# A two-block transformer kernel: Silu tiles that wait for the slots they overwrite, a time-step chain moved up, another order in the first pair, and products of constants in four waits

## The chip, the cores and the metric

The kernel runs on one core of one Trainium2 chip. The metric is device time in microseconds, median of the runs. All data is float32. The engines are named as the profile names them: PE multiplies matrices (PEld is its loading of weights), DVE and POOL do elementwise work, ACT evaluates functions, SP issues most DMAs.

## The reference

512 latent tokens and 256 context tokens of width 1024 go through two blocks. The first has two layers: a hybrid mixer (attention beside a state-space scan in two directions) and a gated feed-forward, then a short convolution and a second feed-forward. The second block has an RWKV-7 mix beside dilated attention, a cross attention to a memory, and a last feed-forward. The parts that the change touches:

```python
def ssd_mixer(p, conv_w, conv_b, dt_bias, a_log, d_skip, ssm_norm, h0_f, h0_b):
    z = p[..., IDX_Z:IDX_XBC]
    xbc = jax.nn.silu(dw_conv(p[..., IDX_XBC:IDX_DT], conv_w, conv_b))
    ...
    dt = jax.nn.softplus(p[..., IDX_DT:].astype(jnp.float32).reshape(b, t, 2, SSM_HEADS)
                         + dt_bias.astype(jnp.float32))
    a = -jnp.exp(a_log.astype(jnp.float32))

def ssd_scan(xs, dt, a, bm, cm, h0):
    ...
    a_cs = jnp.cumsum(dtc * a.astype(f32).reshape(g, e), axis=2).transpose(0, 3, 4, 1, 2)
    xdt = x * dtc[..., None]
    cb = jnp.einsum('bclgn,bcsgn->bcgls', cc, bc)
    y_diag = jnp.einsum('bcgls,bgecls,bcsgep->bclgep', cb, segsum_exp(a_cs), xdt)
    decay_to_end = jnp.exp(a_cs[..., -1:] - a_cs)
    ...

def rwkv7_mix(p_r, p_k, p_v, p_wd, p_ad, p_gd, w0, w2, a0, a2, g2, k_k, k_a, r_k, gn_w, gn_b):
    ...
    kk = kk / jnp.maximum(jnp.sqrt(jnp.sum(kk * kk, axis=-1, keepdims=True)), 1e-12)
    k = p_k * (1.0 + (a - 1.0) * k_a)
    y = rwkv7_scan(r, decay, k, v, -kk, kk * a)
    ...
    bonus = (jnp.sum(r * k * r_k, axis=-1, keepdims=True) * v).reshape(B, S, RWKV_DIM)
```

## The kernel before, in words

Everything is one function, `two_blocks`, with one hand-written program per engine. An engine runs its program in order; a wait names another engine's step (a counter that a `prog` object keeps), so the order of lines is the order of work, and an engine that waits holds up all that stands behind it. Weights come through a ring of four slots that SP fills ahead.

**Attention loop and state-space lead.** Attention takes 16 steps (4 head pairs by 4 query tiles). Between its own operations each step carries fill: PE does projections, DVE convolves tiles of the state-space input (`convolution`, six tiles of 768 columns) and multiplies rows of the modulation weights (`ada_unit`, L2574, 80 units; their rows arrive in four slots named AW). PE sums each finished block of ten (`block_sums`, L1317), DVE adds a bias (`block_mod`, L2585). Behind the loop comes the lead of the state-space scan. ACT applies Silu to the six convolved tiles (L2222 and L2223, steps s0 to s5). Their destination XS lies on the memory of the AW slots, so before the change all six wait for the last `block_mod`, "b9". Then, all in ACT's order: Silu of the gate z (L2225); the exponentials and the logarithm of the softplus (L2229, L2231, L2233); half of the copies of the transposed tiles (L2236, L2239); the exponentials of the decay sums, dte and dcy (L2241, L2242). DVE has the other steps of softplus (L2683 to L2694: u, d, r, ru, corr, pos; then sp, dt and dta to L2703), its own copies (L2709), the masked products CBM (L2713) and the decay sums (L2716 to L2722). PE waits for s5, then transposes the tiles (tx, L1378; tb, L1383), multiplies the B and C parts (cb, L1392), sums the decays (acs, L1398; tot, L1401) and starts the scan proper with `running` (L1438). POOL moves B and C to other partitions by four DMAs (L1080, after s5).

**First RWKV pair.** Eight head pairs go one after the other. Most of what pair i needs is made during pair i-1; the first has to make it itself (DVE L2973 to L3010): shift mixes, the norm of the keys (nmax, ninv, nk: L2984 to L2988), the decay sums (cs, t, km: L2993 to L2997), the decayed operands (bb, rt, at0, at, bt, kt: L2999 to L3007) and the input of the bonus (rk, L3010). PE waits for rk and then transposes (tr, L1682), makes the gram products, part of a projection (L1636) and the first level of an inverse (p0, L1725). POOL multiplies the grams by level masks (L1123) for p0. Before the first pair POOL also scales the eight tiles of X by `rstd` (L1112), which DVE makes by a reciprocal (L3020) after rk.

**Four places where PE waits for DVE or ACT.** Before the output projection of the hybrid mixer PE waits for the normalized group "y1" (L1502). Behind `scaled_pe` (L748) in the two feed-forwards and in the short convolution it waits for the fourth low part of the normalized input, "l3", and later for "l7" (L848). Before the last feed-forward's second product it waits for the first hidden tiles (`ff2_products`, L833).

Of the kernel before, what the change touches and what calls it, by code (L numbers as in the profile page):

```python
# [295 lines left out]
def two_blocks(nc, a, consts_d, bias_d, out):  # L296

    ctx = ExitStack()
    with ctx:
# [204 lines left out]
        ss_pe = prog("ss_pe", " ".join(f"tx{c}" for c in range(NA)) + " tb0 tb1 cb0 cb1 acs tot")  # L504
# [638 lines left out]
        def _(pe):  # L1143
# [250 lines left out]
            pe.wait_ge(dt_dve.sem, dt_dve.done("dta"))  # L1394
            pe.wait_ge(ss_dve.sem, ss_dve.done("tx3"))
            flat = lambda x: x.rearrange("p d c h -> p d (c h)")
            for d in range(2):
                mm = nc.tensor.matmul(bank[3][:, d * 48:(d + 1) * 48], const["tri_b" if d else "tri_f"], flat(DT["dta"])[:, d, :],  # L1398
                                      start=True, stop=True)
            mm.then_inc(ss_pe.sem, ss_pe.step("acs"))  # L1400
            nc.tensor.matmul(bank[3][:, 96:192], ONES, DT["dta"].rearrange("p d c h -> p (d c h)"),  # L1401
                                        start=True, stop=True).then_inc(ss_pe.sem, ss_pe.step("tot"))
# [1883 lines left out]
```

## Time and profile before

| | us |
|---|---|
| median of 3 runs | 2822.73 |
| lowest and highest | 2822.01, 2824.67 |
| the profiled execution | 2820.58 |
| its span in the trace | 2818.8 |
| PE busy | 2709.2 (96%) |
| share of the chain that ended last | PE 83%, DVE 3%, issue 1%, ACT 1% |

Busy time is summed over instructions of an engine. The chain is followed back from the last instruction to what released each step. PEclk, in the windows view, is the clock that TensorE was granted, as a share of full speed (1.00 is 2.4 GHz, 0.50 is 1.2 GHz). In a timeline, the bracket at the end of a line is the idle time of the engine before that instruction and the engine, tile and line that ended it.

### The profile page before, as it was taken

Reading aid. Unit: us, or ns where it says so; the run is one execution under the profiler, and the core shown is the slowest. Engines: PE = TensorE matmul, PEld = TensorE weight load, DVE = VectorE, ACT = ScalarE, POOL = GpSimd, SP = SyncE. Lnnn points to the kernel's source line nnn. Section 1 sums busy time; section 2 is a strip of 40 time slices with the busy share of each in tenths; the row PEclk is TensorE's granted clock in tenths of the full one; section 3 lists DMA queues with packets and bytes.
Section 4 is the critical chain, followed back from the end, with each engine's and each line's share of the span. In section 5 each row is a group of like instructions: output and inputs, shape, how many; then the busy total and the mean of one; then the engine's idle time right before and its main releaser. Section 6 shows DMA issues by size and latency. Waiting matters only on the chain.

```text
span 2818.8 us, 43450 instructions
## 1 busy us (share of the span) xinstructions
PE 2709.2 (96%) x17761; PEld 1956.3 (69%) x17761; DVE 1663.6 (59%) x2208; ACT 655.8 (23%) x1138; POOL 202.9 (7%) x219
## 2 busy tenths in 40 slices
PE   7899799999999999999989999999989999999998
PEld 4555455888878878888645555575667788788887
DVE  4788676555456665554456666654365675655554
ACT  4233433111010021110133333232341211211102
POOL 2000231000000010000031111110000000100001
PEclk9999899999999999999999999999999999999999
DMA  7475302333323323333211211112123333233332
GB/s 256 150 260 189 100 23 82 97 89 95 95 86 97 90 86 93 97 93 95 70 38 34 58 42 34 34 57 65 43 56 89 91 106 111 68 97 94 93 96 74
DMA packets 394393, 255.53 MB, mean 91 GB/s; under 512 B 19767, under 2 KB 376720, under 8 KB 394128
## 3 DMA queue, kind: packets, MB, share of 16 engines
q1 hardware_dynamic: 391456, 246.78, 29.6%
q0 software_dynamic: 2320, 5.11, 0.6%
q8 instruction: 107, 1.75, 0.3%
q10 hardware_dynamic: 480, 1.64, 0.2%
q14 instruction: 30, 0.25, 0.0%
HBM read 250.61 MB, written 2.10 MB: 90 GB/s over the span
## 4 chain that ended last, share of the span: by engine, by line
PE 83%; DVE 3%; issue 1%; ACT 1%; POOL 0%; DVEq 0%; ACTq 0%; POOLq 0%
PE PS L833 15%; PE PS L834 15%; PE PS L835 15%; PE PS L1636 5%; PE PS L849 3%; PE PS L848 3%; PE PS L1611 3%; PE PS L850 3%; PE PS L1725 1%; PE PS L1617 1%; PE PS L1421 1%; PE PS L1502 1%; PE PS L1841 1%; PE PS L1863 1%; PE PS L1751 1%
## 5 line engine op out<-in xcount | busy, mean ns | idle before, releaser
L859 DVE CAST WH<-W 128x1024 fp32r<-128x1024 f32 x304 | 213.4, 702 | 419.0 <-PE PS L835 373.2
L834 PE MATMUL PS<-XNL,WH 128*128 128x512 f32 x960 | 381.8, 398 | 0.0
L861 DVE TENSOR_TENSOR WL<-W,WH 128x1024 fp32r<-128x1024 f32 x304 | 374.5, 1232 | 10.4
L833 PE MATMUL PS<-HH,WH 128*128 128x512 f32 x672 | 262.1, 390 | 0.2 <-DVE HL L2934 0.2
L834 PE MATMUL PS<-HL,WH 128*128 128x512 f32 x672 | 261.5, 389 | 0.0
L835 PE MATMUL PS<-HH,WL 128*128 128x512 f32 x672 | 261.5, 389 | 0.0
L834 PEld LDWEIGHTS PS<-XNL,WH 128*128 128x128 f32 x960 | 180.8, 188 | 41.6 <-issue 0.5
L833 PE MATMUL PS<-XNH,WH 128*128 128x512 f32 x512 | 202.2, 395 | 0.0
L835 PE MATMUL PS<-XNH,WL 128*128 128x512 f32 x512 | 201.3, 393 | 0.0
L833 PE MATMUL PS<-XN2H,WH 128*128 128x512 f32 x448 | 178.6, 399 | 11.4 <-issue 7.5
L835 PE MATMUL PS<-XN2H,WL 128*128 128x512 f32 x448 | 177.5, 396 | 0.0
L1636 PE MATMUL PS<-HXF,W 128*128 128x512 f32 x336 | 165.6, 619 | 0.0
L848 PE MATMUL PS<-XNH,WH 128*128 128x512 f32 x384 | 154.1, 401 | 10.4 <-DVE XNL L779 10.4
L849 PE MATMUL PS<-XNL,WH 128*128 128x512 f32 x384 | 154.0, 401 | 0.0
L850 PE MATMUL PS<-XNH,WL 128*128 128x512 f32 x384 | 152.7, 398 | 0.0
L833 PEld LDWEIGHTS PS<-HH,WH 128*128 128x128 f32 x672 | 126.1, 188 | 28.1 <-DVE HL L3253 1.3
L835 PEld LDWEIGHTS PS<-HH,WL 128*128 128x128 f32 x672 | 126.1, 188 | 26.3
L834 PEld LDWEIGHTS PS<-HL,WH 128*128 128x128 f32 x672 | 126.1, 188 | 26.0
L3043 DVE TENSOR_TENSOR ARENA<-ARENA,PS 128x512 f32<-128x512 f32 (+1 forms) x80 | 48.0, 632 | 117.2 <-PE PS L1753 116.9
L833 PEld LDWEIGHTS PS<-XNH,WH 128*128 128x128 f32 x512 | 96.3, 188 | 23.7 <-issue 0.2
L835 PEld LDWEIGHTS PS<-XNH,WL 128*128 128x128 f32 x512 | 96.2, 188 | 23.0
L833 PEld LDWEIGHTS PS<-XN2H,WH 128*128 128x128 f32 x448 | 85.0, 190 | 35.4 <-issue 15.4
(516 smaller groups left out, 4639.2 us busy)
## 6 DMA issues: line engine op xcount, KB each, us to landing
ARENA<-in_ada_w SPq DMA_DIRECT2D x80, 512.0 KB, 5.3
W<-in_ffn_w SPq DMA_DIRECT2D x64, 512.0 KB, 4.0
W<-in_w_in SPq DMA_DIRECT2D x51, 512.0 KB, 4.0
W<-in_ffn_w_gate SPq DMA_DIRECT2D x44, 512.0 KB, 3.8
W<-in_ffn_w_up SPq DMA_DIRECT2D x44, 512.0 KB, 3.8
W<-in_ffn_w_down SPq DMA_DIRECT2D x32, 512.0 KB, 4.0
W<-in_sc_w_in SPq DMA_DIRECT2D x24, 512.0 KB, 3.8
ARENA<-in_ada_w SPq DMA_DIRECT2D x8, 1024.0 KB, 18.3
```

The costliest lines, as they stand in the source:

```text
L833: nc.tensor.matmul(dst, WH[:, h, c], hi(k), start=(start and k == 0), stop=False)
L834: nc.tensor.matmul(dst, WH[:, h, c], lo(k), start=False, stop=False)
L835: mm = nc.tensor.matmul(dst, WL[:, h, c], hi(k), start=False, stop=(stop and k == kts - 1))
L848: nc.tensor.matmul(dst[u], WH[:, h, c], hi(k), start=(k == 0), stop=False)
L849: nc.tensor.matmul(dst[u], WH[:, h, c], lo(k), start=False, stop=False)
L850: mm = nc.tensor.matmul(dst[u], WL[:, h, c], hi(k), start=False, stop=(k == KD - 1))
L859: nc.vector.tensor_copy(WH[:, h, :], W[:, s, 0:D]).then_inc(parted, 1)
L861: nc.vector.tensor_tensor(WL[:, h, :], W[:, s, 0:D], WH[:, h, :], ALU.subtract).then_inc(freed[s], 1)
L1421: mm = nc.tensor.matmul(bank[6 + o], tiles(sl)[:, NPAIR * o + k, :], MIX[:, k, :], start=(k == 0), stop=(k == NPAIR - 1))
L1611: return nc.tensor.matmul(bank[7], w, xn(k), start=(k == 0), stop=(k == KD - 1))
L1636: mm = nc.tensor.matmul(bank[7], tiles(s)[:, k, :], xn(k), start=(k == 0), stop=(k == KD - 1))
L3043: tt(own, own, PS[:, 2 + 2 * e + first:4 + 2 * e, 0:NT * CHUNK], ALU.add).then_inc(p_dve.sem, p_dve.step(f"z{l}{e}"))
```

## The change

It has three parts.

In the lead, each Silu tile waits for the AW slots that it overwrites (all their uses done) in place of "b9". Tiles 0 to 2 stand ahead of the copy of the last pair's attention output on ACT, 3 to 5 behind it. The softplus chain is spread over the loop: its first DVE steps stand behind the first row maximum, two exponentials on ACT in step 14, six DVE steps and the logarithm in step 15, the rest before the last `block_mod`. PE makes acs and tot, in another bank, before the last `block_sums`; the first transposes wait for s3 alone.

```diff
-        ss_pe = prog("ss_pe", " ".join(f"tx{c}" for c in range(NA)) + " tb0 tb1 cb0 cb1 acs tot")
+        ss_pe = prog("ss_pe", "acs tot " + " ".join(f"tx{c}" for c in range(NA)) + " tb0 tb1 cb0 cb1")
...
+            pe.wait_ge(dt_dve.sem, dt_dve.done("dta"))
+            flat = lambda x: x.rearrange("p d c h -> p d (c h)")
+            for d in range(2):
+                mm = nc.tensor.matmul(bank[7][:, d * 48:(d + 1) * 48], const["tri_b" if d else "tri_f"], flat(DT["dta"])[:, d, :],
+                                      start=True, stop=True)
+            mm.then_inc(ss_pe.sem, ss_pe.step("acs"))
...
             for b in ended(STEPS):
                 block_sums(b, NPAIR)
-            pe.wait_ge(cv_act.sem, cv_act.done(f"s{XBC_TILES - 1}"))
-            pe.wait_ge(at_act.sem, at_act.done(f"o{NPAIR - 1}"))
-            pe.wait_ge(blocks_dve.sem, blocks_dve.done(f"b{len(ADA_BLOCKS) - 1}"))
+            pe.wait_ge(cv_act.sem, cv_act.done(f"s{NPAIR - 1}"))
...
+            def conv_out(j):
+                act.wait_ge(cv_dve.sem, cv_dve.done(f"c{j}"))
+                for u in range(TA * j // D, min((TA * (j + 1) - 1) // D + 1, AW_SLOTS)):
+                    act.wait_ge(aw_used[u], KD * len(ADA_BLOCKS) // AW_SLOTS)
+                nc.scalar.activation(XS[:, j, 0:T], CONV[j][:, 0:T], ACT.Silu, bias=col("conv_b", j))
+                nc.scalar.activation(XS[:, j, T:TA], CONV[j][:, T + 2:TA + 2], ACT.Silu, bias=col("conv_b", j)).then_inc(cv_act.sem, cv_act.step(f"s{j}"))
...
+                if g == STEPS - 1:
+                    act.wait_ge(dt_dve.sem, dt_dve.done("u"))
+                    nc.scalar.activation(act_flat("l"), act_flat("u"), ACT.Ln).then_inc(dt_act.sem, dt_act.step("l"))
+                    act.wait_ge(at_dve.sem, at_dve.done(f"p{STEPS - 1}1"))
+                    for j in range(XBC_TILES // 2):
+                        conv_out(j)
```

On ACT, at the end of the attention loop, this stood in a row before (L2216 copies the last pair's attention output, L2222 and L2223 are Silu of one tile, L2225 Silu of the gate, L2229 to L2233 the softplus, L2236 and L2239 copies of transposed tiles, L2241 and L2242 dte and dcy):

```order
L2222 ACTIVATE ARENA<-ARENA,COLS 128x512
L2223 ACTIVATE ARENA<-ARENA,COLS 128x256
L2225 ACTIVATE ARENA<-ARENA 128x2048
L2229 ACT_TABLE_LOAD
L2229 ACTIVATE ARENA<-ARENA 128x16
L2231 ACTIVATE ARENA<-ARENA 128x96
L2233 ACT_TABLE_LOAD
L2233 ACTIVATE ARENA<-ARENA 128x96
L2236 ACTIVATE HXF<-PS 128x512 x3
L2239 ACTIVATE ARENA<-PS 128x512
L2239 ACTIVATE ARENA<-PS 128x256
L2241 ACT_TABLE_LOAD
```

and this stands there now (L2247 the logarithm, L2216 and L2217 Silu of tiles 2 and 3, L2253 the copy of the attention output, L2258 Silu of the gate, L2261 and L2262 dte and dcy, L2265 copies):

```order
L2247 ACT_TABLE_LOAD
L2247 ACTIVATE ARENA<-ARENA 128x96
L2216 ACT_TABLE_LOAD
...
L2216 ACTIVATE ARENA<-ARENA,COLS 128x512
L2217 ACTIVATE ARENA<-ARENA,COLS 128x256
L2253 ACTIVATE ARENA<-PS 128x512
L2216 ACTIVATE ARENA<-ARENA,COLS 128x512
L2217 ACTIVATE ARENA<-ARENA,COLS 128x256
...
L2258 ACTIVATE ARENA<-ARENA 128x2048
L2261 ACT_TABLE_LOAD
L2261 ACTIVATE ARENA<-ARENA 128x96
L2262 ACTIVATE ARENA<-PS 128x96
L2265 ACTIVATE HXF<-PS 128x512 x3
```

The softplus and two table loads are gone from behind the Silu tiles, and dte and dcy stand ahead of the copies. On PE the same place read before (L1348 values of the last pair):

```order
L1348 MATMUL PS<-ARENA 64x512 x12
L1317 MATMUL PS<-CONST,ARENA 128x2 x8
L1378 MATMUL PS<-CONST,ARENA 128x128 x24
L1383 MATMUL PS<-CONST,ARENA 128x128 x6
L1392 MATMUL PS<-HXF 128x128 x8
L1398 MATMUL PS<-ARENA,CONST 128x48 x2
L1401 MATMUL PS<-ARENA,CONST 128x96
L1438 MATMUL PS<-ARENA,CONST 128x512 x2
```

and now:

```order
L1352 MATMUL PS<-ARENA 64x512 x12
L1377 MATMUL PS<-ARENA,CONST 128x48 x2
L1380 MATMUL PS<-ARENA,CONST 128x96
L1321 MATMUL PS<-CONST,ARENA 128x2 x8
L1388 MATMUL PS<-CONST,ARENA 128x128 x24
L1396 MATMUL PS<-CONST,ARENA 128x128 x6
L1405 MATMUL PS<-HXF 128x128 x8
L1443 MATMUL PS<-ARENA,CONST 128x512 x2
```

The two decay sums moved from behind the B and C products to ahead of the block sums.

In the first RWKV pair, DVE makes cs, t and km ahead of the key norm, PE's transposes wait for kt in place of rk, and `rstd` goes to a place of its own in DIL0, so that POOL can scale X later: one tile behind each pair's level masks.

```diff
-            pool.wait_ge(one_dve.sem, one_dve.done("rstd"))
-            for k in range(KD):
-                nc.gpsimd.tensor_tensor(X[:, k, :], X[:, k, :], YR[:, 2, :], ALU.mult).then_inc(one_pool.sem, one_pool.step(f"x{k}"))
+            def scaled(k):
+                pool.wait_ge(one_dve.sem, one_dve.done("rstd"))
+                nc.gpsimd.tensor_tensor(X[:, k, :], X[:, k, :], DIL0[:, 7, :], ALU.mult).then_inc(one_pool.sem, one_pool.step(f"x{k}"))
...
-            with pool.Fori(0, RW_PAIRS - 1) as i:
+            for i in range(RW_PAIRS - 1):
                 level_masks(i, i, rw_pe, rw_dve, rw_pool)
+                scaled(i)
+            for k in range(RW_PAIRS - 1, KD):
+                scaled(k)
...
                 if i == 0:
-                    pe.wait_ge(rf_dve.sem, rf_dve.done("rk"))
+                    pe.wait_ge(rf_dve.sem, rf_dve.done("kt"))
...
+            decay_sums(0, 0, rf_act, rf_dve)
             key_norm(0, rf_act, rf_dve)
-            decayed(0, 0, rf_act, rf_dve)
+            decayed(0, rf_act, rf_dve)
```

POOL's order at the first pair was (L1109 sums, L1112 scales a tile of X, L1123 a level mask inside a loop of seven pairs):

```order
L1109 TENSOR_TENSOR ARENA<-ARENA 128x512 x6
L1112 TENSOR_TENSOR X<-X,ARENA 128x512 x8
L1126 UNCONDITIONAL_BRANCH
L1126 ISA
L1120 ISA
L1123 TENSOR_TENSOR ARENA<-ARENA,CONST 128x256
```

and is, without the loop:

```order
L1109 TENSOR_TENSOR ARENA<-ARENA 128x512 x6
L1124 TENSOR_TENSOR ARENA<-ARENA,CONST 128x256 x10
L1113 TENSOR_TENSOR X<-X,ARENA 128x512
L1124 TENSOR_TENSOR ARENA<-ARENA,CONST 128x256 x10
L1113 TENSOR_TENSOR X<-X,ARENA 128x512
```

All eight scalings have left the place ahead of the first pair's masks.

Third, PE gets products of constants whose results nobody reads, into banks that are free there: six before the wait for y1, six behind `scaled_pe` in each feed-forward and in the short convolution, seven before the last feed-forward's second product. Each is a float32 product of 512 columns, which PE runs as two halves.

```diff
+            def warm(b, n):
+                for _ in range(n):
+                    nc.tensor.matmul(bank[b], ONES, const["chunk_reset"], start=True, stop=True)
...
+            warm(2, 6)
             pe.wait_ge(gn_dve.sem, gn_dve.done("y1"))
...
                 scaled_pe(pe, norm_ffn[layer], SQ_MIX2, 6)
+                warm(5, 6)
...
             scaled_pe(pe, norm_sc, SQ_MIX2, 6)
+            warm(7, 6)
...
+            warm(3, 7)
             ff2_products(0, True)
```

## Rows read from the trace of the kernel before

**Rows 1.** Page, part 1: busy us, share of the span and instructions of each engine.
```profile
PE 2709.2 (96%) x17761; PEld 1956.3 (69%) x17761; DVE 1663.6 (59%) x2208; ACT 655.8 (23%) x1138; POOL 202.9 (7%) x219
```
**Rows 2.** Timeline of PE in the lead: start, us, engine, line, op, count, idle before.
```profile
305.28 1.95 PE L1317 MATMUL PS<-CONST,ARENA 128*128 128x2 f32 x16 [0.69 <-ACT ARENA L2216]
315.02 5.38 PE L1378 MATMUL PS<-CONST,ARENA 128*128 128x128 f32 x24 [7.79 <-ACT ARENA L2223]
...
322.46 2.02 PE L1392 MATMUL PS<-HXF 64*128 64x128 f32 x16 [0.99 <-DVE HXF L2709]
...
327.19 3.78 PE L1438 MATMUL PS<-ARENA,CONST 128*128 128x512 f32 x4 [1.26 <-ACT ARENA L2242]
```
**Rows 3.** Timeline of ACT in the lead.
```profile
296.97 0.81 ACT L2203 ACTIVATE ARENA<-PS 128x768 f32<-128x768 f32 x1 [1.70 <-PE PS L1306]
...
307.50 1.28 ACT L2222 ACT_TABLE_LOAD   x1 [2.27 <-DVE MOD L2585]
308.80 0.72 ACT L2222 ACTIVATE ARENA<-ARENA,COLS 128x512 f32<-128x512 f32 x1
...
314.87 1.89 ACT L2225 ACTIVATE ARENA<-ARENA 128x2048 f32<-128x2048 f32 x1
```
**Rows 4.** Timeline of DVE in the lead.
```profile
296.55 4.05 DVE L2574 SCALAR_TENSOR_TENSOR ARENA<-ARENA,SILU_C 128x1024 f32<-128x1024 f32 x3
...
323.63 2.48 DVE L2713 TENSOR_TENSOR ARENA<-PS,CONST 128x512 f32<-128x512 f32 x4
```
**Rows 5.** Timeline of POOL in the lead; then the tile view of HXF, from issue to landing.
```profile
315.57 2.09 POOL L1080 DMA_DIRECT2D HXF<-ARENA  x4 [297.49 <-ACT ARENA L2223]
...
DMA to landing us min/median/max: 2.6/3.6/4.1
```
**Rows 6.** Windows: us, then PE, PEld, DVE, ACT, POOL busy (instructions), PEclk, DMA share, GB/s.
```profile
302.00:307.00 5.00, 4.31 (x30) 2.33 (x24) 0.00 (x0) 0.60 (x1) 0.00 (x0) 1.00 0.36 87
315.00:321.00 6.00, 5.98 (x28) 5.98 (x29) 2.19 (x8) 5.94 (x9) 2.09 (x4) 0.50 0.53 131
318.50:320.70 2.20, 2.20 (x12) 2.20 (x12) 1.92 (x7) 2.19 (x4) 0.00 (x0) 0.50 0.64 168
```
**Rows 7.** Timeline of DVE in the first RWKV pair.
```profile
1431.31 0.43 DVE L2984 TENSOR_SCALAR RSTD<-ROOT 128x512 f32<-128x512 f32 x1 [2.69 <-ACT ROOT L2321]
...
1435.77 1.22 DVE L2993 TENSOR_TENSOR_SCAN ARENA<-CONST,ARENA 128x512 f32<-128x512 f32 x1
...
1438.01 0.69 DVE L2999 SCALAR_TENSOR_TENSOR ARENA<-ARENA 128x512 f32<-128x512 f32 x1
...
1441.22 0.75 DVE L3010 SCALAR_TENSOR_TENSOR ARENA<-ARENA,COLS 128x512 f32<-128x512 f32 x1
...
1451.99 1.75 DVE L3036 TENSOR_TENSOR ARENA<-ARENA,CONST 128x512 f32<-128x512 f32 x1
```
**Rows 8.** Timeline of PE: the first pair, and the transposes of the second and third.
```profile
1442.02 3.67 PE L1682 MATMUL PS<-CONST,ARENA 128*128 128x128 f32 x16 [4.68 <-DVE ARENA L3010]
...
1456.73 1.38 PE L1725 MATMUL PS<-ARENA 64*64 64x64 f32 x32 [2.78 <-POOL ARENA L1123]
...
1511.02 1.91 PE L1682 MATMUL PS<-CONST,ARENA 128*128 128x128 f32 x16
...
1572.76 1.91 PE L1682 MATMUL PS<-CONST,ARENA 128*128 128x128 f32 x16
```
**Rows 9.** Timeline of POOL in the first pair.
```profile
1445.31 10.77 POOL L1112 TENSOR_TENSOR X<-X,ARENA 128x512 f32<-128x512 f32 x8 [20.61 <-DVE ARENA L3020]
```
**Rows 10.** Timeline of PE at the waits that get products of constants.
```profile
416.72 3.65 PE L1502 MATMUL PS<-ARENA,W 128*128 128x512 f32 x4 [3.55 <-DVE ARENA L2735]
...
454.54 0.76 PE L848 MATMUL PS<-XNH,WH 128*128 128x512 f32 x1 [3.46 <-DVE XNL L779]
...
459.51 0.50 PE L848 MATMUL PS<-XNH,WH 128*128 128x512 f32 x1 [0.29 <-DVE XNL L779]
...
2449.37 0.76 PE L833 MATMUL PS<-XN2H,WH 128*128 128x512 f32 x1 [3.88 <-DVE XNL L753]
```

More of the change, by code:

```diff
@@ L1369, in _ @@
                     values(g // NT)
+            pe.wait_ge(dt_dve.sem, dt_dve.done("dta"))
[4 more added lines that the diff above has]
+            mm.then_inc(ss_pe.sem, ss_pe.step("acs"))
+            nc.tensor.matmul(bank[7][:, 96:192], ONES, DT["dta"].rearrange("p d c h -> p (d c h)"),
+                                        start=True, stop=True).then_inc(ss_pe.sem, ss_pe.step("tot"))
             for b in ended(STEPS):
                 block_sums(b, NPAIR)
-            pe.wait_ge(cv_act.sem, cv_act.done(f"s{XBC_TILES - 1}"))
-            pe.wait_ge(at_act.sem, at_act.done(f"o{NPAIR - 1}"))
-            pe.wait_ge(blocks_dve.sem, blocks_dve.done(f"b{len(ADA_BLOCKS) - 1}"))
+            pe.wait_ge(cv_act.sem, cv_act.done(f"s{NPAIR - 1}"))
             for c in range(NA):
@@ L1380, in _ @@
             for c in range(NA):
+                if c == 0:
+                    pe.wait_ge(cv_act.sem, cv_act.done(f"s{NPAIR}"))
+                    pe.wait_ge(blocks_dve.sem, blocks_dve.done(f"b{len(ADA_BLOCKS) - 1}"))
                 if c == 4:
@@ L1393, in _ @@
                 mm.then_inc(ss_pe.sem, ss_pe.step(f"cb{g}"))
-            pe.wait_ge(dt_dve.sem, dt_dve.done("dta"))
             pe.wait_ge(ss_dve.sem, ss_dve.done("tx3"))
[L1396 to L1402, printed above, removed]
             pe.wait_ge(dt_act.sem, dt_act.done("dcy"))
@@ L1736, in pair_pass @@
                     if l == 4:
+                        if i == 0:
+                            pe.wait_ge(rf_dve.sem, rf_dve.done("rk"))
                         if ahead:
@@ L2198, in _ @@
                     exps(g + 1)
+                if g + 2 == STEPS:
+                    act.wait_ge(dt_in, 48)
+                    nc.scalar.activation(ALOG, ALOG, ACT.Exp).then_inc(dt_act.sem, dt_act.step("aexp"))
+                    act.wait_ge(dt_dve.sem, dt_dve.done("abs"))
+                    nc.scalar.activation(act_flat("e"), act_flat("abs"), ACT.Exp).then_inc(dt_act.sem, dt_act.step("e"))
                 for e in range(2):
@@ L2239, in _ @@
                 nc.scalar.activation(BTOK[:, 4 * n:4 * n + w, :], bank[b][:, 0:w * P].rearrange("p (c t) -> p c t", t=P), ACT.Copy).then_inc(ss_act.sem, ss_act.step(f"tb{n}"))
-            act.wait_ge(dt_dve.sem, dt_dve.done("tot"))
-            nc.scalar.activation(act_flat("dte"), act_flat("corr"), ACT.Exp).then_inc(dt_act.sem, dt_act.step("dte"))
-            nc.scalar.activation(act_flat("dcy"), bank[3][:, 96:192], ACT.Exp).then_inc(dt_act.sem, dt_act.step("dcy"))
             def group_square(j):
@@ L2706, in _ @@
             dve.wait_ge(dt_dve.sem, dt_dve.done("dta"))
+            dve.wait_ge(ss_pe.sem, ss_pe.done("tot"))
+            nc.vector.tensor_copy(fl("acs"), bank[7][:, 0:96]).then_inc(dt_dve.sem, dt_dve.step("acs"))
+            dve.wait_ge(dt_dve.sem, dt_dve.done("acs"))
+            ts(fl("neg"), fl("acs"), -1.0, None, ALU.mult).then_inc(dt_dve.sem, dt_dve.step("less"))
+            tt(fl("corr"), bank[7][:, 96:192], fl("acs"), ALU.subtract).then_inc(dt_dve.sem, dt_dve.step("tot"))
+            dve.wait_ge(dt_dve.sem, dt_dve.done("tot"))
+            for b in ended(STEPS):
+                block_mod(b)
             for c in range(1, NA, 2):
@@ L2714, in _ @@
                 ins.then_inc(ss_dve.sem, ss_dve.step(f"cb{g}"))
-            dve.wait_ge(ss_pe.sem, ss_pe.done("tot"))
-            nc.vector.tensor_copy(fl("acs"), bank[3][:, 0:96]).then_inc(dt_dve.sem, dt_dve.step("acs"))
-            dve.wait_ge(dt_dve.sem, dt_dve.done("acs"))
-            ts(fl("neg"), fl("acs"), -1.0, None, ALU.mult).then_inc(dt_dve.sem, dt_dve.step("less"))
-            tt(fl("corr"), bank[3][:, 96:192], fl("acs"), ALU.subtract).then_inc(dt_dve.sem, dt_dve.step("tot"))
-            dve.wait_ge(dt_dve.sem, dt_dve.done("tot"))
             dve.wait_ge(dt_act.sem, dt_act.done("dcy"))
```

86 lines of the change are left out of this document (42 added, 44 removed).

## The prediction, made before the changed kernel ran

> **What bounds the kernel now.** I read the page's first part, then the chain of waits, then engine timelines around the touched places, and for each place the granted clock. PE is busy 96% of the span, ACT 23% [rows 1], so only places where PE stands still can give much, and what another engine saves counts only if PE waits for it. There are three sorts here. In the lead, PE finishes its block sums at 305.28 + 1.95 = 307.2, stands 7.79 us until the last Silu tile, and starts the scan (`running`) at 327.19 after a short row of dependent steps [rows 2]. At the first RWKV pair it stands 4.68 us for rk, and 2.78 us before p0 for POOL's mask [rows 8]. At the five places where constant products go in, it stands 3 to 4 us each [rows 10]; of these rows the feed-forward's stands for three places alike (two feed-forwards and the short convolution).
>
> **Part 1, the lead.** The Silu tiles start at 308.80, behind a table load that began when DVE's block_mod (b9) ended [rows 3]. Six tiles take 314.87 - 308.80 = 6.07, 1.01 each. ACT's previous operation ended at 296.97 + 0.81 = 297.8, so nearly 10 us were there to use.
>
> Now I lay the new order on the same clock. The logarithm goes behind 297.8: a table load of 1.28 and about 0.3 (an estimate from the 0.27 per small operation below), so 299.4; the next load, for Silu, ends at 300.7. On DVE six softplus steps stand ahead of the last three rows of modulation: in the window of rows 6 that holds them seven small operations are busy 1.92, 0.27 each, with their gaps 2.1 for six. The rows, which ended at 296.55 + 4.05 = 300.6 [rows 4], end at 302.7. Tiles 0 and 1 overwrite slots that are free by 301.4 (a row is 1.35), tile 2 waits for the third of these rows at the latest, so tile 2 is done at 303.7. Then comes the copy that released the block sums at 305.28 (PE waited 0.69 for it [rows 2], thus a copy of some 0.6 from 304.6). It is not delayed, with 0.9 to spare. Tiles 3, 4 and 5 end at 306.2, 307.3 and 308.3.
>
> PE: dta is ready at 302.7 + 3 or 4 small steps = 303.7, so acs and tot start when the values end, 304.6. Before the change they filled PE from the end of cb (322.46 + 2.02 = 324.48) to the start of its 1.26 us wait for `running` (325.93) [rows 2], so 1.45. Then the block sums, 1.95, to 308.0; by then s3 is there, so the transposes start at 308.0 in place of 315.02 with no wait at all. Between 302 and 307 the clock was at 1.00 [rows 6], and PE no longer stops, so I take full speed: 28 of the 30 took 5.98 at 0.50 in 315 to 321 [rows 6]; all 30 at full speed are 3.2, so tx and tb end near 311.2, the last two of tb a little later, because ACT must first copy tx0.
>
> That copy stands behind the gate's Silu (308.3 + 1.89), a table load and two small exponentials: 312.0. Later than all this are the four DMAs of POOL. They began 0.7 after the last Silu tile made way for the gate's [rows 3, 5]; their issue takes 2.09 and landing 2.6 to 4.1 [rows 5]. From s5 at 308.3 this gives 309.0 + 2.09 + 2.6 = 313.7 at the earliest and 315.2 at the latest; the landing of an earlier one can hide in the issue of the next, so I take 313.7. The cb products, 2.02, end at 315.7, and DVE's masked products, 2.48 for four from 323.63 on, ended 326.11 - 324.48 = 1.6 behind cb before [rows 2, 4]. So `running` can start at 317.3 where it was 327.19: **9.9 saved**. What follows keeps its distances, since dte, dcy and the copies are ready earlier still.
>
> What loses its cover: the two exponentials in step 14 and the four small DVE steps at the start of the loop are 0.27 each. ACT is idle most of the loop, DVE stands there waiting for its first exponential; 0 to 1.6 us, I take 0. The most the lead gives: 11.8, if PE also runs `running` at full speed (3.78 for four halves at low clock, 1.9 at full). The least: 7.3 or 5, in the first two rivals.
>
> **Part 2, the first pair.** cs, t and km took 1438.01 - 1435.77 = 2.24 between nk and bb; DVE stood 2.69 before nmax [rows 7], and their inputs are there earlier than the root. So bb starts 2.24 sooner. kt ends where rk starts, 0.6 before the transposes began (1441.22 against 1442.02, less the signal): together the transposes start 2.24 + 0.6 = 2.84 sooner, at 1439.2. Then POOL: eight scalings of 10.77 [rows 9] stood ahead of the first mask, which released p0 at 1456.73. Without them, the pair has no reason to be longer than the next: from the transposes to the next transposes, 1572.76 - 1511.02 = 61.74, against 1511.02 - 1442.02 = 69.00 in the first. That is 7.26 more, **10.1 in all**. The scalings, 1.35 each, fall behind each pair's last mask, when POOL has nothing else for most of the pair; `rstd` must be ready only then. Price 0, at most the third rival's.
>
> **Part 3, constant products.** One half of 512 columns is 3.65/4 = 0.91 at low clock [rows 10], 0.46 at full. Twelve halves are 5.5 against a stand of 3.55, so y1's consumer starts 1.95 late. But it starts at full clock: its four halves cost 1.8 where they cost 3.65. Sum -0.1 to 0.1. In the feed-forwards and the short convolution they end 5.5 - 3.46 = 2.0 late, and PE there soon waits for l7 again: at 459.51 it stood 0.29 for DVE [rows 10], so a late start that catches up by its faster clock ends at the same moment. Three times 0. Before the last feed-forward 14 halves, 6.4 against 3.88: 2.5 late, with as much to win back from the cold clock (0.76 for its first matmul). Sum of part 3: **0**; bounds: -2, if the faster clock carries further, and +10.7, if none of the clock comes back (5.5 - 3.55, three times 2.0, and 2.5, to 10.5). It lies near 0 because the clock at 1.00 before each place is what the products find.
>
> **Sum.** 9.9 + 10.1 + 0 = 20.0 off the profiled execution's 2820.58: 2800.6. The median stands 2.15 above that execution, so I give **2802.7**.
>
> **Rivals.** *The clock is low where I took it full.* In the lead it stayed at 0.50 through six us of transposes [rows 6], after a stand, and I have no row with thirty transposes behind matmuls. At low clock tx and tb take 6.4, to 314.4, cb ends between 316.4 (full) and 318.4 (low), `running` starts 1.6 later, so the lead gives 9.2 to 7.2. In the pair, PE still stands about 2 us (1442.02 - 4.68 to 1439.2); if the clock falls there, the transposes take 3.67 in place of 1.91 [rows 8] and some grams behind them are slow too, 2.6 in all (estimate). Together 14.7 to 16.7 in place of 20.0: 2806 to 2808, I say 2807. For it: the low row. Against it: the sixteen transposes at 1.91 in the later pairs, behind matmuls. The Trainium skill, "TensorE: Matmul & The Clock Gate", section "Part 4: PE-mode transpose", says that transposes do not count as busy PE, so that the fast clock does not engage for them; by that rule the time would be the one of this rival, some 4 us above mine. The trace agrees with it in the lead, where thirty transposes ran at 0.50, and not in the later pairs, where sixteen ran at the speed of the full clock.
>
> *A later wait eats half of the lead's gain.* Tile 2 waits for the last row of modulation, the copy of the attention output stands behind it on ACT, and PE's block sums behind that; or the DMAs land late. If DVE's rows end 3 us later than I have it, or landing takes 4.1 and the copies slip, the lead gives 5: 9.9 - 5 = 4.9 more, 2807.6. For it: ACT is in order. Against it: 0.9 to spare.
>
> *POOL's scalings disturb DVE.* DVE's L3036 took 1.75 while POOL scaled; like operations on 512 columns take 0.69 [rows 7]. If each moved scaling hits one DVE step on PE's path, seven times 1.06: 2810. Against it: the scaling comes after the last mask, when DVE waits for PE.
>
> *Slower: constant products run at low clock.* If such products do not hold the clock, a half costs 0.91. There are 12 + 36 + 14 = 62, and the five stands hold 3.55 + 3 x 3.46 + 3.88 = 17.8 us. At 0.91 they take 56.4, 38.6 too much; less 20.0 is 18.6 slower, 2841. It decides from 0.61 a half (17.8 + 20.0 over 62). Against it: PE goes into them straight from matmuls, without the stand that went ahead of the low 0.91 [rows 10].
>
> *The change does less than it says.* Were the last uses of the slots as late as b9, the Silu tiles would stay where they are; at nothing for the lead 10.1 is left, 2812.6. Rows 4 speak against it: the last use ends at 300.6, b9 comes after 307.2.
>
> **Chances.** Forecast 0.50; low clock 0.27; later wait 0.10; POOL 0.05; part 3 costing more than it returns, 2806 to 2813, 0.03; slower 0.04; less than it says 0.01. Range: from 2797 (11.8 in the lead and -2 in part 3 are 2798.8, and the sum is good to 2) to 2811, which holds all but the last two and a bit of part 3. A measurement tells about 0.2%, 5.6 us: faster than 2817.1 is 0.93, within 0.03, slower 0.04.
>
> **What would show it.** The trace after should have: the Silu tiles from 301 on, three ahead of the attention copy; no PE stand between the block sums and the transposes; `running` near 317 by the old times; PEclk at 1.00 from 308 to 311; transposes of the first pair 2.8 sooner after its projection and p0 9 us behind them with no POOL release; the second pair's transposes 20 us sooner than before; PE starting 2 us late but at 1.00 at y1 and at the last feed-forward. I am wrong if PE stands for tx at s3, if the DMAs release cb after 315, or if clock after the constant products is 0.50.

## The result, and the profile after

| | us |
|---|---|
| before, median of 4 runs | 2822.37 (2820.93 to 2824.67) |
| the change, median of 4 runs | 2803.22 (2798.78 to 2807.57) |
| ratio, 95% interval | 0.993 (0.9915 to 0.9945) |
| span of the profiled execution, before and after | 2818.8 and 2805.8 |

The change is faster by 19.2 us, with an interval of 15.5 to 24; forecast was 2802.7. The profiled execution of the change is the slowest of its four runs, 2807.57. A second series of the same kernel, told below, gave 0.9914 (0.9901 to 0.9927). Two of the twelve executions of e3_const, below, took 5244 and 8280 us and stand in neither its median nor its ratio.

The page of the changed kernel, first the busy time of the engines and then the chain that ended last:

```profile
PE 2724.9 (97%) x17823; PEld 1961.1 (70%) x17823; DVE 1663.4 (59%) x2208; ACT 653.8 (23%) x1137; POOL 202.0 (7%) x219
...
PE 84%; DVE 3%; ACT 1%; issue 1%; DMA 0%; DVEq 0%; ACTq 0%
```

PE has 62 instructions more than in [rows 1], the halves of the constant products. DMA is new in the chain.

The lead, timeline of PE in the changed kernel (answers to [rows 2]):

```profile
301.66 7.93 PE L1352 MATMUL PS<-ARENA 128*64 128x512 f32 x24 [0.95 <-issue]
309.52 0.65 PE L1377 MATMUL PS<-ARENA,CONST 128*128 128x48 f32 x4
...
310.28 1.95 PE L1321 MATMUL PS<-CONST,ARENA 128*128 128x2 f32 x16
312.09 2.82 PE L1388 MATMUL PS<-CONST,ARENA 128*128 128x128 f32 x24
...
317.33 0.44 PE L1396 MATMUL PS<-CONST,ARENA 128*128 128x128 f32 x2 [1.99 <-ACT HXF L2265]
319.56 2.94 PE L1405 MATMUL PS<-HXF 64*128 64x128 f32 x16 [1.79 <-DMA HXF<-ARENA]
324.15 3.54 PE L1443 MATMUL PS<-ARENA,CONST 128*128 128x512 f32 x4 [1.65 <-DVE ARENA L2750]
```

There is no stand (idle time of PE) between the block sums (310.28) and the transposes (312.09), where 7.79 us stood before. New are waits behind them: 1.99 for ACT's copy of tx0, 1.79 for the DMAs. This run reached the last values (L1352) 3.8 us later than the run of before did, whose row is:

```profile
297.88 6.72 PE L1348 MATMUL PS<-ARENA 128*64 128x512 f32 x24 [0.95 <-issue]
```

So the lead is measured from there: to `running` 29.31 before (297.88 to 327.19) and 22.49 now (301.66 to 324.15), **6.8 shorter**.

ACT and POOL in the same stretch (answers to [rows 3, 5]):

```profile
302.87 0.28 ACT L2247 ACTIVATE ARENA<-ARENA 128x96 f32<-128x96 f32 x1
...
304.47 0.72 ACT L2216 ACTIVATE ARENA<-ARENA,COLS 128x512 f32<-128x512 f32 x1
...
309.63 0.60 ACT L2253 ACTIVATE ARENA<-PS 128x512 f32<-128x512 f32 x1 [2.02 <-PE PS L1352]
...
313.16 1.90 ACT L2258 ACTIVATE ARENA<-ARENA 128x2048 f32<-128x2048 f32 x1
```

```profile
313.85 2.08 POOL L1080 DMA_DIRECT2D HXF<-ARENA  x4 [295.77 <-ACT ARENA L2217]
```

Three Silu tiles stand ahead of the attention copy, which waits for PE and not for them (2.02 idle). The last of the four DMAs was issued at 313.85 + 2.08 = 315.93, and cb started at 319.56, 3.6 later. In the trace the four landed 2.6, 3.4, 3.8 and 4.1 after their own starts, the last at 319.52.

The clock in the windows view of the changed kernel (columns as in [rows 6]):

```profile
302.00:307.00 5.00, 5.00 (x14) 1.51 (x12) 4.60 (x7) 4.96 (x8) 0.00 (x0) 0.51 1.22 237
...
311.00:314.00 3.00, 3.00 (x29) 3.00 (x30) 1.06 (x4) 3.00 (x6) 0.15 (x1) 1.00 0.02 5
```

Between 302 and 307 the clock was mostly low and in the transposes it was full, the other way round than before [rows 6].

The first pair, timelines of PE, POOL and DVE in the changed kernel (answers to [rows 7 to 9]):

```profile
1426.76 7.03 PE L1649 MATMUL PS<-HXF,W 128*128 128x512 f32 x16
1435.68 1.97 PE L1695 MATMUL PS<-CONST,ARENA 128*128 128x128 f32 x16 [1.89 <-DVE ARENA L3042]
...
1497.48 1.69 PE L1695 MATMUL PS<-CONST,ARENA 128*128 128x128 f32 x14
```

```profile
1441.36 1.24 POOL L1124 TENSOR_TENSOR ARENA<-ARENA,CONST 128x256 f32<-128x256 f32 x2 [20.23 <-DVE ARENA L3062]
...
1461.17 1.26 POOL L1113 TENSOR_TENSOR X<-X,ARENA 128x512 f32<-128x512 f32 x1
```

```profile
1457.91 1.28 DVE L3079 TENSOR_TENSOR ARENA<-ARENA,PS 128x512 f32<-128x512 f32 x2 [1.02 <-PE PS L1768]
1463.05 1.29 DVE L3079 TENSOR_TENSOR ARENA<-ARENA,PS 128x512 f32<-128x512 f32 x2 [3.86 <-PE PS L1768]
```

The projection of before, whose transposes began at 1442.02 [rows 8]:

```profile
1430.32 7.03 PE L1636 MATMUL PS<-HXF,W 128*128 128x512 f32 x16
```

From the projection to the transposes it is 8.92 us now and was 11.70: 2.78 less. From these transposes to the second pair's 61.80, before 69.00: 7.20 less. Together **10.0**. POOL has its masks ready at 1442.6, and scales its first tile from 1461.17 on, while DVE stands idle.

The constant products, timelines of PE in the changed kernel (answers to [rows 10]):

```profile
409.56 5.42 PE L1506 MATMUL PS<-CONST 128*128 128x512 f32 x12
414.81 1.88 PE L1512 MATMUL PS<-ARENA,W 128*128 128x512 f32 x4
416.52 1.88 PE L1414 MATMUL PS<-ARENA,CONST 128*128 128x512 f32 x4
...
446.28 1.12 PE L748 MATMUL PS<-HXF,CONST 128*128 128x512 f32 x2 [0.97 <-ACT HXF L732]
447.24 5.31 PE L1506 MATMUL PS<-CONST 128*128 128x512 f32 x12
...
455.84 0.50 PE L848 MATMUL PS<-XNH,WH 128*128 128x512 f32 x1 [0.30 <-DVE XNL L779]
...
2432.71 6.17 PE L1506 MATMUL PS<-CONST 128*128 128x512 f32 x14
2438.31 0.80 PE L833 MATMUL PS<-XN2H,WH 128*128 128x512 f32 x1
```

The group squares and L748 in the kernel before:

```profile
420.20 1.88 PE L1409 MATMUL PS<-ARENA,CONST 128*128 128x512 f32 x4
...
449.95 1.13 PE L748 MATMUL PS<-HXF,CONST 128*128 128x512 f32 x2 [0.97 <-ACT HXF L732]
```

At y1 the end of the work ahead to the group squares takes 416.52 - 409.56 = 6.96; before, 413.17 (416.72 - 3.55) to 420.20 is 7.03. In the feed-forward, from L748 to the wait for l7, 9.56 both times (before 449.95 to 459.51). In the last feed-forward, from the last product ahead of the wait to L748 behind it, 12.7 and before 13.1. A half costs 5.42/12 = 0.45.

### The profile page after: what moved, and what is told of

It reads as the page before. It is cut to its first block, busy times and chain, and to the rows that moved or that the text cites. A ratio compares the mean times of both kernels' runs of the same rounds, so it can differ in the third digit from the quotient of the medians.

```text
span 2805.8 us, 43507 instructions
## 1 busy us (share of the span) xinstructions
PE 2724.9 (97%) x17823; PEld 1961.1 (70%) x17823; DVE 1663.4 (59%) x2208; ACT 653.8 (23%) x1137; POOL 202.0 (7%) x219
## 4 chain that ended last, share of the span: by engine, by line
PE 84%; DVE 3%; ACT 1%; issue 1%; DMA 0%; DVEq 0%; ACTq 0%
PE PS L834 15%; PE PS L833 15%; PE PS L835 15%; PE PS L1649 5%; PE PS L849 3%; PE PS L848 3%; PE PS L850 3%; PE PS L1624 3%; PE PS L1738 1%; PE PS L1630 1%; PE PS L1856 1%; PE PS L1426 1%; PE PS L1512 1%; PE PS L1878 1%; PE PS L1766 1%
```

## Experiments

The lead's length is that from the last values' start to `running` in each profile. "The change" below has two series: 0.993 and 0.9914.

| label | ratio to before, 95% interval | median, before of its series | values, `running` | lead |
|---|---|---|---|---|
| before | | | 297.88, 327.19 | 29.3 |
| the change | 0.9930 (0.9915 to 0.9945) | 2803.22, 2822.37 | 301.66, 324.15 | 22.5 |
| e1_lead | 0.9979 (0.9970 to 0.9988) | 2815.30, 2820.61 | 296.86, 319.29 | 22.4 |
| e2_pair | 0.9959 (0.9947 to 0.9972) | 2808.26, 2820.61 | | |
| e3_const | 0.9998 (0.9987 to 1.0008) | 2820.89, 2820.61 | | |
| e4_lead_pair | 0.9944 (0.9932 to 0.9957) | 2803.45, 2820.61 | | |
| e5_hold | 0.9943 (0.9929 to 0.9957) | 2801.63, 2821.05 | | |
| e6_bc | 0.9921 (0.9907 to 0.9934) | 2799.44, 2821.05 | 295.94, 316.81 | 20.9 |
| e7_bc_z | 0.9921 (0.9907 to 0.9934) | 2799.19, 2821.05 | 299.69, 320.87 | 21.2 |
| e8_b9 | 0.9957 (0.9943 to 0.9970) | 2809.94, 2821.05 | 296.59, 324.24 | 27.7 |
| e9_step15 | 0.9914 (0.9901 to 0.9927) | 2799.79, 2824.91 | 296.94, 316.99 | 20.1 |
| e10_best | 0.9919 (0.9906 to 0.9932) | 2801.72, 2824.91 | 294.83, 317.63 | 22.8 |
| e11_pool | 0.9943 (0.9930 to 0.9956) | 2809.29, 2824.91 | | |
| e12_after | 0.9914 (0.9901 to 0.9927) | 2800.48, 2824.91 | 295.78, 317.93 | 22.2 |

### The three parts, each alone, and two together

e1_lead is the kernel before with the change's lead alone; e2_pair with the first pair's order and POOL's scalings alone; e3_const with the constant products alone; e4_lead_pair is the change without these:

```diff
-            warm(2, 6)
...
-                warm(5, 6)
...
-            warm(7, 6)
...
-            warm(3, 7)
```

> Only the lead (Silu waits, softplus and decay sums moved). Theory: the lead alone is worth what the changed trace shows between the last pair's values and the scan's start, 6.8 us where the clock is low at both ends and up to the forecast 9.9 where it is full: 2812.5 to 2816 beside 2822.4 before, with the b and c products released by the DMAs. Rival (the gain is eaten by a later wait on the Silu slots): 5 or less, 2817.5 or more.

> Only the first RWKV pair (order of the decay sums, transposes after kt, the eight scalings of X behind the pairs' masks). Theory: 10.0, of which 2.8 by the time of the first transposes and 7.2 by the second pair's: 2812.4 beside 2822.4. Rival (POOL's scalings disturb DVE in seven pairs): about 3, 2819.

> Only the products of constants, 62 halves of some 0.45 us. Theory: PE starts its next work 2 us late at each of five places and wins it back by the full clock, in sum 0.5 to 1 less: 2821.5 to 2822. Rival (the clock that they hold is worth nothing, as DVE sets the pace there): some 10 more, 2833. Second rival (the clock is worth more than the trace shows at the five places): 3 or more less, 2819 or lower.

> The change without the products of constants. Theory: the parts add, 6.8 to 9.9 for the lead and 10.0 for the pair: 2802.5 to 2805.6, within 1 of the whole change on like runs, and with the same spread of several us between runs, because the spread comes from the clock ahead of the attention loop, which no part touches. Rival (the products of constants carry the clock and with it the gain): 2808 or more.

e1_lead: 3.4 to 8.5 us faster by its interval, 5.3 by the medians. That lies between the theory (6.8 or more) and the rival (5 or less), and the time can't tell them; the lead in its profile is 22.4, 6.9 shorter, and no stand is ahead of its transposes, so the rival's later wait did not come. e2_pair: 8 to 15 faster, where 10.0 were expected, and its transposes again stand 1.89 in place of 4.68. e3_const: 0.6 faster by its ratio, between 3.7 faster and 2.3 slower. This excludes the first rival (10 more); small gains and losses can't be told, and the second rival's 3 less lies inside the interval. e4_lead_pair: 12 to 19 faster. Its 0.9944 lies inside the first series of the change and above the second (0.9901 to 0.9927), so this ratio alone does not show that the constant products carry nothing; its median, 2803.45, is that of the change's first series (2803.22), and e3_const and the rows above have them near 0. The parts' ratios add to 0.9936.

### Products ahead of the attention loop

e5_hold adds eight constant products at four stands ahead of the loop; the first of them:

```diff
+            for _ in range(2):
+                nc.tensor.matmul(bank[1], ONES, lat(0), start=True, stop=True)
             pe.wait_ge(hy_act.sem, hy_act.done("kroot"))
             pe.wait_ge(hy_dve.sem, hy_dve.done("knormed"))
```

> The whole change, and 8 more products of constants (16 halves, 7 us of PE) at four stands of 1.5 to 2.8 us ahead of the attention loop, where PE waits for DVE. Theory: the clock falls by chance after these stands, in some runs and not in others, and that makes the spread of 9 us between runs of one kernel: with the stands filled the low stretches between 90 and 140 us are gone, the attention loop starts 3 to 5 us sooner, the runs lie closer together, and the median is 2 to 5 lower than the change's. Rival (the late start of the loop belongs to the change itself, or products only add time there): same or up to 3 higher.

The reason for it is a late start of the loop in the changed kernel's profile, and one instruction on the way there. PE in the kernel before, in the changed kernel, and in the second series of the changed kernel, behind the same stand of 2.15:

```profile
83.19 1.13 PE L1236 MATMUL PS<-ARENA,CONST 128*128 128x512 f32 x2 [2.15 <-DVE ARENA L2594]
```

```profile
84.58 1.70 PE L1240 MATMUL PS<-ARENA,CONST 128*128 128x512 f32 x2 [2.15 <-DVE ARENA L2621]
```

```profile
81.12 1.13 PE L1240 MATMUL PS<-ARENA,CONST 128*128 128x512 f32 x2 [2.15 <-DVE ARENA L2621]
```

Same code, same stand, but the two halves took 1.70 in one run and 1.13 in the two others; the window 84.5 to 88.5 of the changed kernel has a mean clock of 0.57:

```profile
84.50:88.50 4.00, 3.92 (x6) 1.93 (x7) 2.86 (x5) 0.00 (x0) 0.00 (x0) 0.57 0.69 185
```

So the first profile of the change began its loop late by chance. In all fourteen profiles of this document the two parts go together: where the two halves behind this stand took 1.6 to 1.8 (six profiles) the last values start at 299.7 to 301.7, and where they took 1.12 or 1.13 (eight) at 294.8 to 297.9. The fall behind this stand is not the whole of it: between the change's two profiles the instruction itself already came 3.5 later (84.58 against 81.12), and the clock had been 0.85 from 46 to 62 in the late one and 1.00 from 45 to 59 in the other.

In e5_hold the loop's first scores start at 123.28, at 127.2 in the first profile of the change, and at 121.8 in its second, without any product. Its products do hold the clock where they stand (the two halves behind the second stand take 1.12, where the change's profiles have 1.78 and 1.49), but the last values start at 296.0, and at 295.8 in the second profile of the change. The spread did not go either: five runs from 2800.98 to 2810.24. Theory and rival both fail in part: the late loop is chance and not the change, and filling these four stands gained nothing. The stand of 2.15 lies ahead of all four and was left as it was, so whether it makes the spread between runs was not tested.

### B and C first, and the gate's Silu ahead of the attention copy

```diff
-                    for j in range(XBC_TILES // 2):
+                    for j in (0, 4, 5):
                         conv_out(j)
...
-            for j in range(XBC_TILES // 2, XBC_TILES):
+            for j in (1, 2, 3):
                 conv_out(j)
```

That is e6_bc. e7_bc_z moves the gate's Silu up too:

```diff
                     for j in (0, 4, 5):
                         conv_out(j)
+                    act.wait_ge(at_act.sem, at_act.done(f"e{NPAIR - 2}"))
+                    nc.scalar.activation(ZS, ZS, ACT.Silu).then_inc(zs_act.sem, zs_act.step("silu"))
```

> The whole change with the Silu tiles in the order 0, 4, 5 ahead of the attention copy, then 1, 2, 3: POOL's four DMAs of B and C start some 5 us sooner, at the price that the transposes start 1.2 later. Theory: the DMAs were what ended PE's last wait ahead of the b and c products (1.79 us in the changed trace), and after them ACT's copies are late (they let the last two tb transposes wait 1.99); so about 2.5 less than the change, the copies next. Rival (landing is hidden by the copies anyway): 0 to 0.5 less, or 1 more from the later transposes.

> As the order 0, 4, 5 first, and Silu of the gate also ahead of the attention copy, in ACT's idle 2 us there, so that ACT's copies come 1.9 sooner. Theory: 3.4 less than the change, and the masked products of DVE are what ends the last wait before the scan. Rival (the copy, and with it PE's block sums, is late by the gate's 1.9): 1 more than with the order alone.

PE in e6_bc, timeline:

```profile
306.58 5.38 PE L1388 MATMUL PS<-CONST,ARENA 128*128 128x128 f32 x24 [1.08 <-ACT ARENA L2217]
311.75 1.13 PE L1396 MATMUL PS<-CONST,ARENA 128*128 128x128 f32 x6
312.82 2.05 PE L1405 MATMUL PS<-HXF 64*128 64x128 f32 x16
316.81 3.75 PE L1443 MATMUL PS<-ARENA,CONST 128*128 128x512 f32 x4 [1.95 <-DVE ARENA L2750]
```

The waits for the copy and for the DMAs are gone; cb follows tb with no stand, at the price of 1.08 ahead of the transposes. The lead is 20.9, 1.3 to 1.6 shorter than in the change's two profiles, not 2.5: here the transposes took 5.38 at the low clock, and with the DMAs out of the way that counts. Moving the gate's Silu gave nothing more (21.2; expected 0.9 less), since ACT's copies then waited for PE's slow transposes. In time, 0.9921 for both lies between the change's two series: no difference can be told.

### Silu behind b9 again

```diff
-                    for j in range(XBC_TILES // 2):
-                        conv_out(j)
...
-            for j in range(XBC_TILES // 2, XBC_TILES):
+            act.wait_ge(blocks_dve.sem, blocks_dve.done(f"b{len(ADA_BLOCKS) - 1}"))
+            for j in range(XBC_TILES):
                 conv_out(j)
```

> The whole change, but all six Silu tiles wait for b9 again and stand behind the attention copy; softplus and decay sums stay where the change put them. Theory: the Silu waits carry most of the lead's gain, 5 to 6 of the 7 to 8 us; transposes start near 7 us later than in the change and the rest of the row follows: 5 to 6 more than the change. Rival (softplus and decay sums carry it): 2 more or less.

PE in e8_b9, timeline:

```profile
312.00 4.76 PE L1388 MATMUL PS<-CONST,ARENA 128*128 128x128 f32 x24 [4.51 <-ACT ARENA L2217]
...
320.24 2.05 PE L1405 MATMUL PS<-HXF 64*128 64x128 f32 x16 [1.76 <-DMA HXF<-ARENA]
324.24 3.75 PE L1443 MATMUL PS<-ARENA,CONST 128*128 128x512 f32 x4 [1.94 <-DVE ARENA L2749]
```

A stand of 4.51 is back ahead of the transposes, the lead is 27.7, and the time is 0.9957, above both series of the change (by 0.27% to 0.43%, 7.6 to 12 us; its interval overlaps that of the first). By the leads, the Silu waits carry 5.2 to 5.5 of the 6.8 to 7.2 us, softplus and decay sums 1.7, as expected. The times put it higher, but they can't size it: the span of this profile, 2805.6, is that of the change's first, 2805.8.

### Products in the last attention step

```diff
+                if g == STEPS - 1:
+                    pe.wait_ge(at_act.sem, at_act.done(f"exp{g}1"))
+                    held(3)
                 turn(g, 0)
                 fill(g, range(3, 5))
+                if g == STEPS - 1:
+                    held(1)
                 turn(g, 1)
                 fill(g, range(5, KD))
+                if g == STEPS - 1:
+                    held(1)
```

where `held(n)` issues n constant products into bank 0. That is e9_step15; e10_best has this, the products ahead of the loop, and e7_bc_z's order together.

> The whole change, and five products of constants (10 halves, 4.5 us of PE) in the three stands of PE in the last attention step (2.67 for DVE's weights, 0.99 and 0.95 for ACT). Theory: these stands are why the clock is at 1.2 GHz for 7 to 10 us from the last values on in every profile so far, so that values, transposes or b and c products run slow, each in another run; with the stands filled that low stretch is gone, values take 5.4 in place of 6.7 to 8.2, and the time is 2 to 4 less than the change. Rival (the low stretch lies beside waits for ACT, DVE and the DMAs that end when they end): same within 1, PE only stands longer for the DMAs.

> All that helped, together: the change, Silu order 0, 4, 5 with the gate ahead of the attention copy, products of constants in the stands ahead of the loop and in its last step. Theory: the gains add where the DMAs no longer end the lead: 2793 to 2797, runs within 5 us of each other. Rival (the gains overlap, DVE's masked products set the lead's end): 2798 to 2800.

PE in e9_step15, timeline:

```profile
296.94 5.37 PE L1352 MATMUL PS<-ARENA 128*64 128x512 f32 x24
303.56 0.65 PE L1387 MATMUL PS<-ARENA,CONST 128*128 128x48 f32 x4 [1.25 <-DVE ARENA L2742]
...
306.04 2.82 PE L1398 MATMUL PS<-CONST,ARENA 128*128 128x128 f32 x24
...
312.75 2.59 PE L1415 MATMUL PS<-HXF 64*128 64x128 f32 x16 [1.82 <-DMA HXF<-ARENA]
```

The clock's part holds: values take 5.37, transposes 2.82, and the low stretch is gone until cb. But PE then waits 1.25 for dta and 1.82 for the DMAs. The lead is 20.1, 2.1 shorter than in the second profile of the change, yet PE reaches the values 1.2 later, so `running` comes 0.9 sooner; and the time, 0.9914, is that of the change in the same series. The rival's forecast came, the same within 1. That the low stretch lies mostly beside waits fits the DMAs, whose wait is as long as in the change. In e10_best, for which 2793 to 2797 were expected, PE waits for ACT's attention copy ahead of the block sums. This wait was 0.69 in the kernel before [rows 2], is gone in the change, and was 0.14 in e7_bc_z:

```profile
305.13 3.58 PE L1327 MATMUL PS<-CONST,ARENA 128*128 128x2 f32 x16 [2.77 <-ACT ARENA L2273]
```

Values that end sooner meet a copy that stands behind the gate's Silu, and that behind a Silu tile that waits 1.91 for DVE's modulation row. The lead is 22.8, the time 2801.72, no better than the change and above the 2798 to 2800 of its rival too.

### POOL's scalings back, and the change once more

```diff
-            for i in range(RW_PAIRS - 1):
-                level_masks(i, i, rw_pe, rw_dve, rw_pool)
-                scaled(i)
-            for k in range(RW_PAIRS - 1, KD):
+            for k in range(KD):
                 scaled(k)
+            for i in range(RW_PAIRS - 1):
+                level_masks(i, i, rw_pe, rw_dve, rw_pool)
```

That is e11_pool; e12_after is the change itself.

> The whole change, but POOL scales all eight tiles of X ahead of the first pair's masks again. Theory: p0 of the first pair waits for POOL's 10.8 us again and comes 6.6 to 7.3 later; with the clock that falls in that wait 7 to 8.5 more than the change, so the order of DVE's steps alone is worth 2.8. Rival (the order made DVE ready so much earlier that POOL ends in time): 3 or less.

> The change itself once more, beside the others on one chip. Theory: 2799 to 2808, with the low stretches of the clock ahead of the loop and in the lead lying differently from profile to profile, and the first pair as in the first profile.

PE in e11_pool, then in e12_after, timelines:

```profile
1432.12 2.53 PE L1694 MATMUL PS<-CONST,ARENA 128*128 128x128 f32 x16 [1.89 <-DVE ARENA L3041]
1447.46 1.97 PE L1737 MATMUL PS<-ARENA 64*64 64x64 f32 x32 [4.43 <-POOL ARENA L1124]
...
1503.01 1.91 PE L1694 MATMUL PS<-CONST,ARENA 128*128 128x128 f32 x16
```

```profile
1427.83 1.96 PE L1695 MATMUL PS<-CONST,ARENA 128*128 128x128 f32 x16 [1.90 <-DVE ARENA L3042]
...
1437.11 1.15 PE L1738 MATMUL PS<-ARENA 64*64 64x64 f32 x32
```

From the transposes to p0 15.34 against 9.28, 6.1 more, and the time 8.8 more by the medians of one series; expected 7 to 8.5. From these transposes to the second pair's it is 70.9 against 61.8, 9.1 more, which is all of it; p0 took 1.97 in place of 1.15. So the moved scalings are worth nearly all of the pair's gain. That the order alone is worth 2.8, as expected, does not come out: from the projection (1423.20) to the second pair's transposes e11_pool takes 79.8, and the kernel before 80.7 (1430.32 to 1511.02), 0.9 more. With the scalings ahead of the masks p0 waits for POOL, and transposes that come sooner only make it wait longer (4.43 in place of 2.78). The old pair took 81.7 and 81.8 in the profiles of e1_lead and e3_const, so up to 2.0 of the order's worth is possible.

In e12_after the lead looks otherwise than in the first profile and ends almost alike (22.2):

```profile
305.02 4.48 PE L1388 MATMUL PS<-CONST,ARENA 128*128 128x128 f32 x24
...
312.50 3.78 PE L1405 MATMUL PS<-HXF 64*128 64x128 f32 x16 [1.81 <-DMA HXF<-ARENA]
317.93 3.75 PE L1443 MATMUL PS<-ARENA,CONST 128*128 128x512 f32 x4 [1.65 <-DVE ARENA L2750]
```

Transposes of 4.48 in place of 2.82 cost nothing, because cb waits for the DMAs in both; cb's 3.78 in place of 2.94 does cost.

## Why the prediction was right, step by step

**The lead: right mechanism, too large.** 9.9 were forecast, 6.8 to 7.2 are there. From the end of the values to `running` I had 304.6 to 317.3, 12.7; the two profiles of the change have 14.6 (309.52 to 324.15) and 15.5 (302.45 to 317.93). The step that failed is the DMAs' landing: of 2.6 to 4.1 I took the earliest end on the ground that earlier ones hide in later issues, but it is the last one that counts. The 2.6 is the landing of the first DMA; the last landed 4.1 after its own start, 3.6 after the end of its issue, in both profiles and before the change too, 1.0 more than I had. And cb, which I priced at 2.02, ran at a mean clock of 0.67 and of 0.50 behind that wait, 2.94 and 3.78, so 0.9 and 1.8 more. That makes up the 1.9 and 2.8. The other 1.2 that the first profile's 6.8 lacks are values that ran slow ahead of it (7.93 for 6.72). The order of events came as forecast: three tiles ahead of the copy, no stand ahead of the transposes, DVE's masked products as the last wait, 1.65.

**The first pair: right in all its terms.** Transposes 2.78 sooner (2.84 forecast), pair 7.20 shorter (7.26), p0 9.28 behind the transposes (9). The clock stayed full through the stand of 1.89, which was the doubt. The two terms hold only together: e11_pool shows that the first alone gives 0.9, since p0 then waits for POOL.

**Constant products: right.** A half costs 0.45 (0.46), PE starts 1.7 late at y1 and has it back by the group squares; the feed-forward's wait for l7 ends at the same moment, and the last feed-forward has 0.4 more back than it lost. Their sum by the rows is within half a microsecond of 0, e3_const's 0.9998 agrees. Two sums beside the forecast are off: the upper bound of this part adds to 10.5 and not 10.7, and the chances of a time below 2817.1 to 0.96 and not 0.93.

**The rivals.** The low clock in the transposes came in one of the change's two profiles and not in the other, and it mattered in neither. The Trainium skill, "TensorE: Matmul & The Clock Gate", section "Part 4: PE-mode transpose", says that the fast clock does not engage for transposes; the trace disagrees here: 24 float32 transposes took 2.82 us at a granted clock of 1.00 behind matmuls, and 5.38 at 0.50 where the clock had fallen ahead of them. In the second profile of the change (4.48) the clock was 1.00 between 302 and 305 and 0.60 between 305 and 307: it fell in the middle of the transposes, with no stand of PE since the values began. Why is not shown. Of the later wait, the half on the Silu slots did not come (ACT was 2.02 idle ahead of the copy); e10_best shows how little is needed for it. Its other half, DMAs that land late, came by 1.0. POOL's scalings did not disturb DVE: in both profiles of the change seven ran while DVE stood idle, and the eighth beside two DVE operations that took their usual 0.69 and 0.68. That constant products run at low clock was wrong by the factor of two: 0.45.

**What stays open.** The rows give 6.8 to 7.2 + 10.0 + about 0.5, some 17.5. The first series lies at 19.2 with 17.5 inside its interval; the second, 24.4 by the medians and 20.6 to 28 by its interval, lies beyond it. Of the 5.2 between the two, 2.5 is the kernel before (2824.91 in one series, 2822.37 in the other) and 2.7 the change (2800.48 and 2803.22). That the median came within 0.5 of the forecast is partly luck: the sum had 20.0 where the rows show some 17.5. The lengths of the stages in three profiles, by PE's rows, show where the rest lies:

| stage | before | the change, first | second |
|---|---|---|---|
| to the last values | 297.9 | 301.7 | 295.8 |
| the lead, to `running` | 29.3 | 22.5 | 22.2 |
| to the first feed-forward's L748 | 122.8 | 122.1 | 122.8 |
| first feed-forward, to the next L748 | 375.5 | 375.5 | 373.2 |
| to the first pair's projection | 604.9 | 605.0 | 605.0 |
| to the second pair's transposes | 80.7 | 70.7 | 70.7 |
| to the last pair's transposes | 371.0 | 371.0 | 371.0 |
| to the end | 936.8 | 937.3 | 935.3 |

The change's two profiles are 9.9 apart, and hardly any of it lies in the lead or in the pair: 5.9 lies ahead of the last values, 2.3 in the first feed-forward, 2.0 behind the last pair. These are differences between executions and not the change's work. The first feed-forward took 375.5 in seven of the fourteen profiles and 373.1 or 373.2 in seven, with and without constant products. Low clock is not the cause there: it was granted 1.00 through both profiles of the change, and matmuls start 231.3 ns apart on the mean in one and 229.8 in the other. Why a stage takes one pace or the other stays open, and so does what sets the clock ahead of the loop.

## What to carry to other kernels

Wait for the bytes that are overwritten and not for the last event of the stage: here it took away a stand of 7.8 us, but the queue behind it (a copy, then DMAs) was nearly as late, so only 5.2 to 5.5 of it was gain. Look for batches of unhurried work, as POOL's eight scalings, that stand ahead of a small piece for which PE waits; spreading them was worth 9.1 us here, the reordering on DVE 0.9 to 2.0 by itself. And before filling PE's stands to keep its clock, see which wait ends the stretch: where it is a DMA or ACT, as in e9_step15 and e10_best, a faster PE waits all the same. And know the spread: stages of one and the same code differed here by 2 to 6 us from execution to execution, as much as the smaller parts of the change are worth.

## What the runs showed of the hardware

After one and the same stand of 2.13 to 2.15 us the clock fell in six of fourteen profiles and stayed in eight (1.60 to 1.83 against 1.12 or 1.13 for the two halves behind it). After a stand of 1.9 the first pair's sixteen transposes took 1.96 or 1.97 in ten profiles, and 2.53 in e11_pool. At a granted clock of 1.00 the same feed-forward took 375.5 us in one profile of the change and 373.2 in the other, its matmuls 231.3 and 229.8 ns apart throughout. Of four DMAs of 192 KB issued in a row by POOL, 0.5 us apart, the first landed 2.6 us after its start and the last 4.1, before and after the change. Filling PE's stands with products of constants does keep the clock (e9_step15: 5.37 for values that took 6.7 to 8.2 in the kernels without them), at 0.45 a half.
